# Masked softmax steps of 128 query rows: steps with few keys put together two by two in a PSUM bank, and the projection work between the steps dealt out again

## The reference, cut to what matters

```python
# block 1: even_mixer: 8 heads of 64, softmax attention over masked keys, beside a short gated conv
proj = xn @ w_in                       # q, k, v and gate_b, gate_c, h
a = dilated_attention(q, k, v)
b = gate_b * causal_dwconv(gate_c * h, sconv_w)
...
# blocks 3 and 4: hybrid_mixer
o = g[..., 0:1] * o_cmp + g[..., 1:2] * o_slc + g[..., 2:3] * o_win   # 8 heads, 3 branches
o_sb = stick_breaking_attention(q, k, v)                             # 8 heads
g_a, g_b = jnp.split(jax.nn.sigmoid(g_merge), 2, axis=-1)            # g_merge = a part of h @ w_in
y = g_a * (o_nsa @ w_proj_nsa) + g_b * (o_sb @ w_proj_sb)
```

## Time and profile before

| | |
|---|---|
| three runs | 3084.84 us median (3080.89 to 3085.85) |
| the profiled execution, its own time | 3085.91 us |
| its span in the trace | 3084.2 us |
| mean granted TensorE clock | 0.988 |
| TensorE matmul busy | 3027.0 us (98%) |
| DVE, ACT, POOL busy | 1782.5 (58%), 1274.4 (41%), 148.3 us (5%) |
| HBM | 84 GB/s over the span |

### The profile page before, as it was taken

The page is one execution under the profiler, slowest core; times in us unless marked ns, Lnnn a source line. Parts: engine busy times, 40 slices in busy tenths (PEclk is TensorE's granted clock), DMA queues, the critical chain, the costliest instruction groups (busy, mean ns, idle before and its releaser), DMA issues.

```text
span 3084.2 us, 38061 instructions
## 1 busy us (share of the span) xinstructions
PE 3027.0 (98%) x14656; PEld 2399.4 (78%) x14656; DVE 1782.5 (58%) x3231; ACT 1274.4 (41%) x2430; POOL 148.3 (5%) x203
## 2 busy tenths in 40 slices
PE   8999999999999999999999999999999999999998
PEld 7678888888887888888866687888787666878886
DVE  4565875345554487634465567775364655577743
ACT  4344443323233344432365644443232656344431
POOL 0100000000000000001000201000020001010000
PEclk9999999999999999999999999999999999999999
DMA  3222322222222333333211132323232111323332
GB/s 140 75 83 94 103 98 96 96 82 82 82 76 75 96 102 97 96 96 97 89 42 35 38 100 75 103 97 101 83 98 89 35 35 43 102 76 103 96 98 73
DMA packets 71892, 260.36 MB, mean 84 GB/s; under 512 B 8096, under 2 KB 8096, under 8 KB 71584
## 3 DMA queue, kind: packets, MB, share of 16 engines
q1 hardware_dynamic: 70272, 252.67, 25.6%
q10 hardware_dynamic: 1440, 5.26, 0.4%
HBM read 255.81 MB, written 2.10 MB: 84 GB/s over the span
## 4 chain that ended last, share of the span: by engine, by line
PE 93%; DVE 4%; ACT 1%; issue 0%; POOL 0%; ACTq 0%; DVEq 0%; POOLq 0%
PE bank L437 26%; PE bank L440 25%; PE bank L444 25%; PE bank L593 2%; PE bank L514 2%; PE bank L518 2%; PE bank L515 2%; PE bank L623 2%; PE bank L604 1%; PE bank L745 1%; PE bank L862 1%; PE bank L892 1%; PE bank L549 1%; PE bank L734 1%; DVE wl L1312 1%; PE bank L870 1%
## 5 line engine op out<-in xcount | busy, mean ns | idle before, releaser
L1312 DVE TENSOR_TENSOR wl<-ring,wh 128x512 fp32r<-128x512 f32 (+1 forms) x944 | 647.5, 693 | 796.1 <-ACT wh L945 790.7
L437 PE MATMUL bank<-xh,wh 128*128 128x512 f32 x2464 | 994.1, 403 | 17.1 <-ACT wh L945 10.1
L440 PE MATMUL bank<-xh,wl 128*128 128x512 f32 x2464 | 969.0, 393 | 9.5 <-DVE wl L1312 9.4
L444 PE MATMUL bank<-xl,wh 128*128 128x512 f32 x2464 | 928.1, 392 | 0.0
L945 ACT ACTIVATE wh<-ring 128x512 fp32r<-128x512 f32 (+1 forms) x944 | 579.1, 622 | 743.9 <-PE bank L444 668.5
L437 PEld LDWEIGHTS bank<-xh,wh 128*128 128x128 f32 x2464 | 467.3, 190 | 157.9 <-issue 46.1
L440 PEld LDWEIGHTS bank<-xh,wl 128*128 128x128 f32 x2464 | 467.8, 190 | 103.6 <-DVE wl L1312 14.4
L444 PEld LDWEIGHTS bank<-xl,wh 128*128 128x128 f32 x2464 | 466.4, 189 | 99.4
L437 PE MATMUL bank<-bigr,wh 128*128 128x512 f32 x1024 | 399.8, 390 | 4.0 <-ACT wh L945 2.8
L440 PE MATMUL bank<-bigr,wl 128*128 128x512 f32 x1024 | 399.3, 390 | 0.3 <-DVE wl L1312 0.3
L444 PE MATMUL bank<-bigr,wh 128*128 128x512 f32 x1024 | 394.0, 390 | 0.0
(11 more groups left out here) (199 smaller groups left out, 2769.7 us busy)
## 6 DMA issues: line engine op xcount, KB each, us to landing
ring<-in_w_up SPq DMA_DIRECT2D x176, 512.0 KB, 3.5
ring<-in_w_down SPq DMA_DIRECT2D x88, 512.0 KB, 3.5
ring<-in_w_in SPq DMA_DIRECT2D x64, 512.0 KB, 3.5
ring<-in_w_ret SPq DMA_DIRECT2D x32, 512.0 KB, 3.3
ring<-in_w_even SPq DMA_DIRECT2D x20, 512.0 KB, 3.5
ring<-in_w_ret_v SPq DMA_DIRECT2D x16, 512.0 KB, 3.2
ring<-in_w_ret_out SPq DMA_DIRECT2D x16, 512.0 KB, 3.4
ring<-in_w_proj SPq DMA_DIRECT2D x16, 512.0 KB, 3.4
```

The costliest lines, as they stand in the source:

```text
L437: e.matmul(o, K.wh(p, c * 128, 128), oh, start=start, stop=False, skip_group_check=True)
L440: e.matmul(o, K.wl(p, c * 128, 128), oh, start=False, stop=False, skip_group_check=True)
L444: m = e.matmul(o, K.wh(p, c * 128, 128), ol, start=False, stop=stop, skip_group_check=True)
L1312: e.tensor_tensor(K.wl(i, 0, w), K.raw(i), K.wh(i, 0, w).bitcast(F32), ALU.subtract).then_inc(F.lo.tell(("piece", i)), 1)
```

## The change

- A step may now hold two pairs ("parts") whose scores lie side by side in banks 0 and 1: query tiles 2 and 0 (384 + 128 columns) in block 1; in blocks 3 and 4 tiles 2 and 0 of one branch, and tile 1 of both branches (256 + 256). That makes 3 steps in place of 4 for each head pair in block 1 (12 in all) and 5 in place of 8 in blocks 3 and 4 (20 a block). The order of query tiles is now 3, then 2 with 0, then 1. The matmuls and transposes are the same in number and shape, as are the masks, exponentials and scalings; one reciprocal now covers 2 or 4 columns, and one copy out of the transposes' bank covers both parts.
- The fill steps come by functions of t: in block 1 7 for t < 6, then 6, until iteration 14 of 15; in blocks 3 and 4 2 and 3 in turn, 57 in the 23 iterations of `soft`. The other 71 fall to the stick-breaking stage, whose tensor program is not touched.
- `merge_to` in that stage counts from 57 in place of 64.

```diff
-    def den(self, i, a):
-        return self.SM[:, 128 + 4 * (i % 4) + a:129 + 4 * (i % 4) + a]
+    def den(self, t, u, a, n=1):
+
+        at = 128 + 16 * (t % 2) + 4 * a + u
+        return self.SM[:, at:at + n]
...
-Unit = namedtuple("Unit", "q k v mask base qt qready kready vready start stop gate gateready cmp early done out")
-
-
-def even_units(K):
+Unit = namedtuple("Unit", "q k v mask base qt at qready kready vready start stop gate gateready")
+Step = namedtuple("Step", "pairs early cmp done out")
+
+
+def even_steps(K):
 
     out = []
     for j in range(4):
-        for qt in range(NQ):
-            for base in (0, 64):
-                h = 2 * j + base // 64
-                out.append(Unit(K.Q[j], K.Q[4 + j], lambda kt, h=h: K.VT[:, kt * S + h * 64:kt * S + (h + 1) * 64], K.DIL,
-                                base, qt, ("qk", j), ("qk", 4 + j), ("freed", "e", "v", 3), True, True, None, None, None, None,
-                                ("on", "e", j) if qt == 3 else None, K.Q[j]))
+        for qts in ((3,), (2, 0), (1,)):
+            pairs = []
+            for qt, at in zip(qts, (0, 384)):
+                pairs.append([Unit(K.Q[j], K.Q[4 + j], lambda kt, h=2 * j + i: K.VT[:, kt * S + h * 64:kt * S + (h + 1) * 64],
+                                   K.DIL, 64 * i, qt, at, ("qk", j), ("qk", 4 + j), ("freed", "e", "v", 3), True, True, None,
+                                   None) for i in range(2)])
+            out.append(Step(pairs, None, None, ("on", "e", j) if qts == (1,) else None, K.Q[j]))
     return out
 
 
-def nsa_units(K, l):
+def nsa_steps(K, l):
+
 
     out = []
     for j in range(4):
-        for qt in range(NQ):
-            for br in (1, 2):
+        for m, parts in enumerate((((3, 1, 0),), ((3, 2, 0),), ((2, 1, 0), (0, 1, 384)), ((2, 2, 0), (0, 2, 384)),
+                                   ((1, 1, 0), (1, 2, 256)))):
+            pairs = []
+            for qt, br, at in parts:
+                pair = []
                 for kv in range(2):
                     h, v0 = 4 * kv + j, (br - 1) * 128 + 64 * kv
-                    p = len(out) // 2
-                    out.append(Unit(K.NQT[j], (K.KSL, K.KWN)[br - 1], lambda kt, v0=v0: K.TM[:, kt * 280 + v0:kt * 280 + v0 + 64],
-                                    K.cs("causal", 512), 64 * kv, qt, ("rope", l, 1 + j), ("rope", l, 4 + br),
-                                    ("freed", "tm", l, 3), False, br == 2, K.gv[:, qt, 3 * h + br:3 * h + br + 1], ("gates", l),
-                                    j if qt == 0 and br == 1 else None, 0 if p == 0 else j + 1 if p % 8 == 4 and j < 3 else None,
-                                    ("on", l, j) if br == 2 and qt == 3 else None, K.NQT[j]))
+                    pair.append(Unit(K.NQT[j], (K.KSL, K.KWN)[br - 1], lambda kt, v0=v0: K.TM[:, kt * 280 + v0:kt * 280 + v0 + 64],
+                                     K.cs("causal", 512), 64 * kv, qt, at, ("rope", l, 1 + j), ("rope", l, 4 + br),
+                                     ("freed", "tm", l, 3), False, br == 2, K.gv[:, qt, 3 * h + br:3 * h + br + 1],
+                                     ("gates", l)))
+                pairs.append(pair)
+            early = 0 if j == 0 and m == 0 else j + 1 if m == 2 and j < 3 else None
+            out.append(Step(pairs, early, j if m == 0 else None, ("on", l, j) if m == 4 else None, K.NQT[j]))
     return out
+
+
+def width(step):
+
+    return sum((pair[0].qt + 1) * 128 for pair in step.pairs)
+
+
+def fill_even(t):
+
+    return 6 * (t + 1) + min(t + 1, 6)
+
+
+def fill_nsa(t):
+    return 2 * (t + 1) + (t + 1) // 2
 
...
-    def soft(L, units, fill, per):
-
...
-                pair = units[2 * t:2 * t + 2]
-                if pair[0].early is not None:
-                    cmp_turn(L[1], pair[0].early)
-                for i, u in enumerate(pair):
-                    w, r = (u.qt + 1) * 128, slice(u.base, u.base + 64)
-                    q.wait_ge(F.dve, u.qready)
-                    q.wait_ge(F.dve, u.kready)
-                    empty(i)
-                    e.matmul(BK[i][:, 0:w], u.q[r, u.qt * 128:w], u.k[r, 0:w], start=True,
-                             stop=True).then_inc(F.attn.tell(("scores", L, 2 * t + i)), 1)
-                    vacated[i] = [(F.dve, ("top", L, 2 * t + i))]
-            fill(per)
+                if steps[t].early is not None:
+                    cmp_turn(L[1], steps[t].early)
+                for pair in steps[t].pairs:
+                    for i, u in enumerate(pair):
+                        w, r = (u.qt + 1) * 128, slice(u.base, u.base + 64)
+                        q.wait_ge(F.dve, u.qready)
+                        q.wait_ge(F.dve, u.kready)
+                        if pair is steps[t].pairs[0]:
+                            empty(i)
+                        m = e.matmul(BK[i][:, u.at:u.at + w], u.q[r, u.qt * 128:w], u.k[r, 0:w], start=True, stop=True,
+                                     skip_group_check=True)
+                        if pair is steps[t].pairs[-1]:
+                            m.then_inc(F.attn.tell(("scores", L, t, i)), 1)
+                            vacated[i] = [(F.dve, ("top", L, t, i))]
+            each = upto(t) - (upto(t - 1) if t else 0)
+            fill(each - each // 2)
...
                 for i in range(2):
-                    n_ = 2 * (t - 2) + i
-                    u = units[n_]
-                    q.wait_ge(F.dve, ("p", L, n_))
+                    q.wait_ge(F.dve, ("p", L, t - 2, i))
                     empty(2 + i)
-                    for kt in range(u.qt + 1):
-                        m = e.transpose(BK[2 + i][:, kt * 128:(kt + 1) * 128], K.pr(n_)[:, kt * 128:(kt + 1) * 128],
-                                        K.cs("ident"))
-                    m.then_inc(F.attn.tell(("turned", L, n_)), 1)
-                    vacated[2 + i] = [(F.act, ("pt", L, n_))]
-            fill(per)
+                    for pair in steps[t - 2].pairs:
+                        u = pair[i]
+                        for c in range(u.at, u.at + (u.qt + 1) * 128, 128):
+                            m = e.transpose(BK[2 + i][:, c:c + 128], K.pr(2 * (t - 2) + i)[:, c:c + 128], K.cs("ident"))
+                    m.then_inc(F.attn.tell(("turned", L, t - 2, i)), 1)
+                    vacated[2 + i] = [(F.act, ("pt", L, t - 2, i))]
+            fill(each // 2)
...
-                pair = units[2 * t - 6:2 * t - 4]
-                u = pair[0]
+                step = steps[t - 3]
...
-                for kt in range(u.qt + 1):
-                    for i, u in enumerate(pair):
-                        n_ = 2 * (t - 3) + i
-                        q.wait_ge(F.act, ("pt", L, n_))
-                        m = e.matmul(BK[4][u.base:u.base + 64, u.qt * 128:(u.qt + 1) * 128], u.v(kt),
-                                     K.pt(n_)[:, kt * 128:(kt + 1) * 128], start=u.start and kt == 0,
-                                     stop=u.stop and kt == u.qt, skip_group_check=True)
+                    e.matmul(BK[4][:, :], K.vcc, K.cp(step.cmp)[0:64, :], start=True, stop=False,
+                             skip_group_check=True).then_inc(F.attn.tell(("cmpv", L[1], step.cmp)), 1)
+                q.wait_ge(F.act, step.pairs[0][0].vready)
+                for pair in step.pairs:
+                    for kt in range(pair[0].qt + 1):
+                        for i, u in enumerate(pair):
+                            q.wait_ge(F.act, ("pt", L, t - 3, i))
+                            c = u.at + kt * 128
+                            m = e.matmul(BK[4][u.base:u.base + 64, u.qt * 128:(u.qt + 1) * 128], u.v(kt),
+                                         K.pt(2 * (t - 3) + i)[:, c:c + 128], start=u.start and kt == 0,
+                                         stop=u.stop and kt == u.qt, skip_group_check=True)
                 m.then_inc(F.attn.tell(("values", L, t - 3)), 1)
-                if u.done is not None:
-                    half[0] = u.done
+                if step.done is not None:
+                    half[0] = step.done
...
-    soft(("e", 0), even_units(K), fills(steps(("ec", i), DT, xn(s), F.dve) for i in range(12)), 3)
+    soft(("e", 0), even_steps(K), fills(steps(("ec", i), DT, xn(s), F.dve) for i in range(12)), fill_even)
...
-        soft(("n", l), nsa_units(K, l), fill, 1)
+        soft(("n", l), nsa_steps(K, l), fill, fill_nsa)
...
-                for i in (2 * t, 2 * t + 1):
-                    p = K.pr(i)[:, 0:(units[i].qt + 1) * 128]
-                    q.wait_ge(F.dve, ("top", L, i))
-                    e.activation(p, p, ACT.Exp, bias=K.den(i, 0), scale=-1.0, accum_out=K.den(i, 1)).then_inc(
-                        F.act.tell(("exp", L, i)), 1)
+                for part, pair in enumerate(steps[t].pairs):
+                    for i, u in enumerate(pair):
+                        p = K.pr(2 * t + i)[:, u.at:u.at + (u.qt + 1) * 128]
+                        q.wait_ge(F.dve, ("top", L, t, part, i))
```

(117 more changed lines are left out.)

12 lines of the change are left out of this document (6 added, 6 removed).

## The result

3069.53 us median of five runs (3067.68 to 3069.80), against 3083.68 of before (five runs, 3080.89 to 3085.85): 14.2 us less. The ratio is 0.9954, 95% interval 0.9940 to 0.9969. Forecast: 3073.3, -11.5. The profiled execution took 3069.80 us.

A forecast was written before the change was run, and what follows sets the result against it. TensorE, 98% busy, was taken as the bound. Joining -9.8, moved fills -6.7 and the added wait +5.0 make -11.5: 3085.9 to 3074.4 us, and 3073.3 for the median lying 1.1 below; range 3062 to 3084.

The forecast's parts named there:

- What bounds the kernel: Whole kernel: TensorE bounds it, 98% busy and 93% of the chain, never idle in softmax of blocks 3 and 4.
- rival 4: Softmax stages: joined steps turn late, transposes waiting for DVE's scaling, at most 4.3 us a step; 3097 us, chance 0.10.
- Edits at nothing: Block 1's fills, copies, tile order, weight loads and ACT's split at stage end: no cost; split 0.5 us a block if uncovered.
- Part 1: Softmax stages of blocks 1, 3 and 4: 28 fewer values-and-scores groups at 0.35 us each, 9.8 us saved.
- each pass carries its own 0.10, the second too: Scores in softmax stages: the fixed 0.21 us belongs to each pair of scores, so joining saves none of it.
- rival 2: Scores in softmax stages: joined scores share the fixed 0.21 us, 5.9 us better, 3067.4 us; chance 0.12.
- The values' 0.15 and the following fill's 0.20: Softmax stages: fixed price of a values group and extra on the first fill behind scores, both saved by a joined step.
- Part 2: Stick-breaking tail, blocks 3 and 4: 13 moved fill steps cover idle time and slow clock, 3.35 us a block, 6.7 saved.
- Part 3: Stick-breaking stage: ACT's conversion waits for the third fill, second z 0.25 us late in ten iterations, 5.0 us lost.

The follow-up runs named there:

- e4: Kernel after with the joining undone (steps of one part in their old order, fills dealt as in after): 3084.39 us, ratio 1.0004 to before.
- e1: Kernel after with one fill step put between the scores of the two parts in the 28 joined steps: 3077.32 us, ratio 0.9983 to before.
- e6: Kernel after with one fill step put between the values of the two parts in the 28 joined steps: 3076.93 us, ratio 0.9977 to before.
- e3: Kernel after with 69 fill steps in place of 57 in blocks 3 and 4's softmax stages, leaving the stick-breaking tail without fills: 3072.01 us.
- e2: Kernel after with merge_to in the stick-breaking stage counting 3 fill steps fewer, in ACT and DVE programs: 3062.03 us, ratio 0.9934 to before.

## Why the prediction was right, and where it missed

**What bounds the kernel:** right. No wait of TensorE is listed in a softmax stage after the change, though DVE has four maxima in a joined step; rival 4 did not come. (Its 4.3 us of DVE work a step can't be followed from its rows; measured, DVE works 15.7 in the 24.8 us window of some five steps, 3.1 a step.) Block 1 gave 0.46 a group by the difference between e4 and after, less than 0.56. That the rest goes to its tail, where values now stand between fills, was not traced.

**Edits at nothing:** one of them has a price. ACT's split at the end of the stage was called just covered, at 0.5 us a block if not. TensorE does not wait for the split itself, but ACT's later work is late by 0.6 and TensorE loses 0.6 us a block, 1.2 in all.

**Part 1, joining:** the direction and the count of 28 were right, the term was mis-sized: 9.8 forecast, 14.8 measured, 0.56 a group in place of 0.35. The step that failed is "each pass carries its own 0.10, the second too". I had the distance between the starts of the two passes of a pair (0.53 for 0.43 of columns), which is what the first pass costs behind its start, and took the second to cost the same. The other 0.10 of the 0.21 lies in front of the first pass, at the change from values. A run of scores pays both once, whatever its number of passes. The joined step shows it: 384 + 128 columns 1.07, one 512-wide pair 1.06, and nothing more between its second, third and fourth pass than their columns take. This is rival 2, given 0.12 and put at 3067.4, to which the measured 3069.5 is nearer than to the forecast. It is also the strict reading of the Trainium skill ("TensorEngine Tiling (Array Packing)", Key Properties: changing the tiling mode drains TensorE) that the prediction set against its rows; e1 and e6 price such changes at 0.38 and 0.34 us a step, and the starts show 0.10 more at each of them and none between two parts, so here the traces agree with it. The values' 0.15 and the following fill's 0.20 were right (e6).

**Part 2, the tail:** the forecast had 17.29 us from z of step 15 to the tiles `y`; by the starts it is 1755.03 - 1737.80 = 17.23. Of the 3.35 a block, e3 confirms 3.1 where the clock falls and 1.5 where it doesn't. In before it fell in both blocks, so the forecast's size holds for before; that it falls each time is not shown.

**Part 3, the added wait:** its mechanism (the order of ACT's queue, the third fill), its iterations and nearly its size (0.27 to 0.32 for 0.25) were right. Two things in it weren't seen. Where a 512-wide z follows, the accumulate waits for DVE anyway, so four of the ten cost nothing (4 x 0.27 a block). And iteration 1 lost 0.5, and four others 0.06 each. The sum by e2 is 2.5 a block for 2.5 forecast: luck, two misses that cancel. The accumulate's wait of 5.4 us left the list partly because the tail has fills, and partly because z came later, not because DVE came earlier: with e2, 2.7 of it are back.

**Sum:** forecast -9.8 for joining and -6.7 + 5.0 = -1.7 for the dealing; by stages -14.8 and -1.8, and behind them +1.2 from the dealing. Part 1 alone was 5.0 short. The difference of the medians (14.2) is smaller than that of the stages (16.6), because everything else took 0.5 back in the profiled executions (1.2 lost to ACT's late work, 0.7 gained in stretches without an edit), and the profiled execution of before is 2.2 us over its median of five. So it is in part luck that the forecast is off by 2.7 us only.

## What to carry to other kernels

When TensorE is never idle, look for what it pays between kinds of matmul: take runs of each kind from the chain of waits, fit a price per instruction and a fixed price, and see where inside the run the fixed price lies (entry, each pass, or exit) before saying what joining two runs saves; the passage out shows only at the next instruction. When work is dealt out anew, recompute by how much the converting engines run ahead of it: three fill steps of lead were worth 5 us here, and the list of waits did not show it, because half of a concurrent pair kept the engine busy. And give covering work to the place where a wait is left, one by one: moving a fill from behind the accumulate to ahead of it gave 4 us. Look behind the stage too: work of another engine that starts when the last dealt piece is done starts later now, and 0.6 us a block went that way.

## What the runs showed of the hardware

- A run of two-pass fp32 scores on 64x128 row tiles took 0.213 us for each 128 columns of a concurrent pair and 0.21 once, at its entry: 0.10 between the values and its first pass, 0.11 between its first pass and its second. Leaving it cost 0.20 on a following 128x128 fill and 0.15 on following transposes (e1: 1.02 for 0.87). Entering values from a fill cost 0.15. Going from a fill to transposes, both 128x128, cost nothing (8 transposes 0.87, 0.11 each).
- Two concurrent z matmuls of 512 columns, the second 0.27 late, took 1.39 in place of 1.11: the delay was paid in full, and no more.
- Idle stretches of 1.7 and 1.9 us were followed by 3.4 us at 1.2 GHz in three of four tails without fills (both of before, one of e3), and in none of the twelve tails with fills. In e3 the fall cost 1.6 us (stages of 101.32 and 99.74).
